# The two mixers of a long block: order of the weight columns, slots of the interleaved threads, buffers of retention's statistics

## What is computed

```
proj = h @ w_in        # hq hf hi hg (4 heads of 128) | rq rk (4 x 32) rv rg (256) | lx ly (256)
log_f = log(lb + (1-lb) sigmoid(hf));  k = (1-lb) sigmoid(-hf);  q = silu(hq) * 128**-0.5
o_hg  = rmsnorm(hgrn2(q, k, hi, log_f)) * silu(hg)          # 4 heads: gated linear recurrence
o_ret = head_groupnorm(retention(rope(rq), rope(rk), rv)) * silu(rg)
xc    = causal_conv4(lx)
o_lru = rg_lru(xc; sigmoid gates from two small matmuls of xc) * gelu(ly)
h    += concat(o_hg, o_ret, o_lru) @ w_out
```

## Time and profile before

| | us |
|---|---|
| time, median of 3 runs (2721.88 to 2722.41) | 2722.36 |
| the profiled execution's own time | 2721.52 |
| its span, first to last instruction | 2719.7 |
| TensorE busy | 2624.5 |
| VectorE busy | 1371.7 |
| ScalarE busy | 1053.1 |
| the mixers' tiles begin at (first, second) | 1354.35, 2041.12 |

### The profile page before, as it was taken

How to read it: one execution, slowest core, us unless ns; L and a number is a source line. 1 busy time by engine, 2 the same in 40 slices (tenths; PEclk the granted TensorE clock), 3 DMA queues, 4 the chain that set the end, 5 groups by cost and what they waited for, 6 DMA issues and landing times.

```text
span 2719.7 us, 42796 instructions
## 1 busy us (share of the span) xinstructions
PE 2624.5 (96%) x18948; PEld 2341.3 (86%) x18948; DVE 1371.7 (50%) x2195; ACT 1053.1 (39%) x1709; POOL 30.7 (1%) x69
## 2 busy tenths in 40 slices
PE   7999999999999999999999999999999899999998
PEld 5776888888877788888888889999998888999998
DVE  4766633324556643332666446555246644655523
ACT  3554522213444442221544344443234434443421
POOL 0000000000000000000000000000000000000000
PEclk9999999999999999999999999999999999999999
DMA  4221222232312122222311222222232122222222
GB/s 164 83 85 63 78 93 93 90 101 74 109 65 76 63 94 94 97 96 88 114 63 48 67 93 91 94 94 84 92 128 79 34 81 90 80 92 94 90 86 74
DMA packets 39467, 236.04 MB, mean 87 GB/s; under 512 B 5248, under 2 KB 7296, under 8 KB 17008
## 3 DMA queue, kind: packets, MB, share of 16 engines
q1 hardware_dynamic: 34336, 213.93, 23.3%
q0 software_dynamic: 3792, 17.26, 1.8%
q10 hardware_dynamic: 1152, 2.10, 0.2%
HBM read 222.65 MB, written 6.42 MB: 84 GB/s over the span
## 4 chain that ended last, share of the span: by engine, by line
PE 85%; DVE 8%; ACT 5%; DMA 1%; issue 1%; SPq 0%; ACTq 0%; DVEq 0%
PE P L505 72%; PE P L593 3%; PE P L615 2%; PE P L512 2%; DVE WL L1741 1%; ACT WH L1194 1%; PE P L870 1%; PE P L627 1%; PE P L641 1%; PE P L670 1%; PE P L956 1%; DVE X L2041 1%; DVE small L2044 1%; DMA X<-in_xT 0%; PE P L846 0%
## 5 line engine op out<-in xcount | busy, mean ns | idle before, releaser
L505 PE MATMUL P<-XH,WL 128*128 128x264 f32 (+2 forms) x3080 | 851.8, 325 | 34.5 <-DVE WL L1741 19.4
L505 PE MATMUL P<-XL,WH 128*128 128x264 f32 (+2 forms) x3080 | 825.4, 317 | 0.0
L505 PE MATMUL P<-XH,WH 128*128 128x264 f32 (+2 forms) x3080 | 823.6, 316 | 0.0
L1741 DVE TENSOR_TENSOR WL<-raw,WH 128x1024 fp32r<-128x1024 f32 (+1 forms) x404 | 483.8, 1201 | 533.8 <-ACT WH L1194 533.3
L1194 ACT ACTIVATE WH<-raw 128x1024 fp32r<-128x1024 f32 (+1 forms) x404 | 418.0, 1038 | 596.5 <-PE P L505 595.7
L505 PEld LDWEIGHTS P<-XH,WL 128*128 128x128 f32 x3080 | 521.6, 189 | 83.5 <-issue 19.0
L505 PEld LDWEIGHTS P<-XH,WH 128*128 128x128 f32 x3080 | 518.8, 189 | 38.3
L505 PEld LDWEIGHTS P<-XL,WH 128*128 128x128 f32 x3080 | 519.3, 189 | 35.3
L2374 DVE SCALAR_TENSOR_TENSOR tmp<-P,PP,tmp 128x527 f32<-128x527 f32 x88 | 67.4, 766 | 198.5 <-ACT tmp L1690 198.5
L505 PE MATMUL P<-GHH,WL 128*128 128x264 f32 x704 | 150.2, 284 | 0.0
L505 PE MATMUL P<-GHH,WH 128*128 128x264 f32 x704 | 149.6, 283 | 0.0
(11 more groups left out here) (335 smaller groups left out, 3460.5 us busy)
## 6 DMA issues: line engine op xcount, KB each, us to landing
raw<-in_wts SPq DMA_DIRECT2D x170, 1024.0 KB, 4.9
raw<-in_wts SPq DMA_DIRECT2D x32, 896.0 KB, 4.7
spill<-X POOLq DMA_DIRECT2D x2, 2112.0 KB, 9.0
X<-spill POOLq DMA_DIRECT2D x16, 264.0 KB, 4.2
tmp<-in_biasT POOLq DMA_DIRECT2D x16, 256.0 KB, 4.3
qswap<-qraw SPq DMA_DIRECT2D x44, 64.0 KB, 2.0
tab<-in_tR POOLq DMA_DIRECT2D x2, 1056.0 KB, 6.1
X<-in_xT ACTq DMA_DIRECT2D x8, 256.0 KB, 13.1
```

The source lines that it names most:

```text
L505: ins = nc.tensor.matmul(P[:, a:a + x1 - x0], wb[:, s, 128 * k:128 * k + 128], xb[:, kx, x0 - c0:x1 - c0], start=start and i == 0, stop=st ...
L1741: nc.vector.tensor_tensor(WL[:, u % NS, 0:length(u)], raw[:, u // 2 % RAW, a:a + length(u)], WH[:, u % NS, 0:length(u)].bitcast(F), ALU.su ...
```

## The change

It moves things and computes the same. The columns of LRU's input (lx0, lx1) are now the first two tiles, those of its output gate (ly0, ly1) stand ahead of head 3's and retention's gates. The heads have 14 steps, the norm's product and the gate's in two of them, and new slots; LRU runs at slots 10 to 60, its gate at 172 to 184; retention's scores have an empty step after the rope, and the gate of retention is a thread of its own, `ret_gate`, at 188 to 206. Retention's values and statistics lie in buffers of the heads (KBs, hK, Qs, hB, hA), with waits for head 3's last use of them. The output projection takes LRU's k-steps first and retention's last. X is loaded back in another order, at events of its own for each tile. The threads are called with `ret_gate` on all three engines (on TensorE it is idle).

```diff
@@ -18,9 +18,9 @@
 
 
 WIDE = ("v0", "v1", "rv")
-MIXER_TILES = [("v0", 20), ("hf1", 8), ("hq1", 8), ("hg1", 8), ("lx0", 8), ("lx1", 8), ("rq0", 8), ("rk1", 8),
-               ("hf2", 8), ("hq2", 8), ("v1", 20), ("hg2", 8), ("hf3", 8), ("hq3", 8), ("rv", 20), ("hg3", 8),
-               ("rg0", 8), ("rg1", 8), ("ly0", 8), ("ly1", 8)]
+MIXER_TILES = [("lx0", 8), ("lx1", 8), ("v0", 20), ("hf1", 8), ("hq1", 8), ("hg1", 8), ("rq0", 8), ("rk1", 8),
+               ("hf2", 8), ("hq2", 8), ("v1", 20), ("hg2", 8), ("hf3", 8), ("hq3", 8), ("rv", 20), ("ly0", 8),
+               ("ly1", 8), ("hg3", 8), ("rg0", 8), ("rg1", 8)]
 
 
 def mixer_column(name):
@@ -206,10 +206,11 @@
                 pass
 
 
-def mixer_threads(hgrn, lru, ret_scores, ret_values, lru_gate):
-
-    return Threads((hgrn(0), 13, 1, 46), (hgrn(1), 13, 46, 90), (hgrn(2), 13, 92, 136), (hgrn(3), 13, 138, 190),
-                   (lru(), 8, 52, 86), (ret_scores(), 5, 74, 108), (ret_values(), 9, 157, 193), (lru_gate(), 3, 190, 204))
+def mixer_threads(hgrn, lru, ret_scores, ret_values, lru_gate, ret_gate):
+
+    return Threads((hgrn(0), 14, 1, 52), (hgrn(1), 14, 54, 96), (hgrn(2), 14, 98, 136), (hgrn(3), 14, 138, 184),
+                   (lru(), 8, 10, 60), (ret_scores(), 6, 78, 114), (ret_values(), 8, 157, 187), (lru_gate(), 3, 172, 184),
+                   (ret_gate(), 3, 188, 206))
 
 
 def one(b):
@@ -340,8 +341,7 @@
         hseq = [X[:, 6 + n, :] for n in range(2)]
         rraw, RQ, RK = (X[:, 0, :], X[:, 1, :]), X[:, 2, :], X[:, 3, :]
         KTr = X[:, 4, 0:512]
-        ro, rsq = (X[:, 4, :], X[:, 5, :]), X[:, 3, :]
-        tmp_rs = [X[:, n, :] for n in range(2)]
+        ro, rsq, tmp_rs = (KBs[0], KBs[1]), (hK, Qs[0]), (hB, hA)
         rgate = (rstd[:, :], tmp[3])
 
         pe_done, act_done, dve_done, pool_done = (semaphore(n + "_done") for n in ("pe", "act", "dve", "pool"))
@@ -476,11 +476,9 @@
                 for h in range(2, 4):
                     pool.wait_ge(*at("ht", l, h - 1))
                     nc.gpsimd.memset(hB[:, :], 1.0).then_inc(*pool.up("hB", l, h))
-                for k in (2, 0, 1, 3, 4, 5, 6, 7):
-                    if k == 2:
-                        pool.wait_ge(*at("rpv", l, 1))
-                    else:
-                        pool.wait_ge(*at("gl", l, max(k, 5)))
+                for k, event in ((0, ("rt", l)), (1, ("rt", l)), (3, ("rt", l)), (5, ("rt", l)), (4, ("rkv", l, 1)), (2, ("rpv", l, 1)),
+                                 (6, ("gl", l, 6)), (7, ("gl", l, 7))):
+                    pool.wait_ge(*at(*event))
                     nc.gpsimd.dma_start(X[:, k, :], spill[:, k, :]).then_inc(x_back[k], 16)
 
 
@@ -1040,6 +1038,7 @@
                     ones_sum(perm_r, rraw[n], two(3), True, True).then_inc(*pe.up("rperm", l, n))
                     give((6, 7), ("rrope1", l, n))
                     yield
+                yield
                 for n in range(2):
                     pe.wait_ge(*at("rrope", l, 1))
                     take(4, 5, 6, 7)
@@ -1106,13 +1105,13 @@
                 for n in range(2):
                     pe.wait_ge(*at("ro", l, n))
                     take(6, 7)
-                    ones_sum(ones_ret, ro[n], two(3), True, True).then_inc(*pe.up("rmean", l, n))
+                    ones_sum(ones_ret, ro[n][:, :], two(3), True, True).then_inc(*pe.up("rmean", l, n))
                     give((6, 7), ("rcen", l, n))
                     yield
                 for n in range(2):
                     pe.wait_ge(*at("rsq", l, n))
                     take(6, 7)
-                    ones_sum(ones_ret, rsq, two(3), True, True).then_inc(*pe.up("rvar", l, n))
+                    ones_sum(ones_ret, rsq[n][:, :], two(3), True, True).then_inc(*pe.up("rvar", l, n))
                     give((6, 7), ("rl", l, n))
                     yield
                 yield
...
@@ -1141,11 +1141,11 @@
                         tile(U + u, two(p), XH, XL, slot)
                         give((2 * p, 2 * p + 1), (name[:2], l, int(name[2])))
                 UO = first[f"mo{l}"]
-                out_first(UO, works, GH, GL, (0, 1, 2, 4, 5, 3), [two(0), two(1)], ("gl", l), 0)
+                out_first(UO, works, GH, GL, (0, 1, 2, 6, 7, 3), [two(0), two(1)], ("gl", l), 0)
 
                 def tiles(m, r):
                     if m < 2:
-                        finish_tile(UO + m, r, GH, GL, (6, 7), ("gl", l), 0)
+                        finish_tile(UO + m, r, GH, GL, (4, 5), ("gl", l), 0)
                     else:
                         tile(UO + m, r, GH, GL)
 
@@ -1567,7 +1567,7 @@
                 yield
 
             def ret_scores(l):
-                for _ in range(4):
+                for _ in range(5):
                     yield
                 act.wait_ge(*at("rt", l))
                 nc.scalar.activation(KTr[:, 0:384], P[:, 2560:2944], ACT.Copy).then_inc(*act.up("rkt0", l))
@@ -1579,23 +1579,27 @@
                 yield
                 for n in range(2):
                     act.wait_ge(*at("rpv", l, n))
-                    nc.scalar.activation(ro[n], pair_bank(3), ACT.Copy).then_inc(*act.up("ro", l, n))
-                    yield
-                act.wait_ge(*at("rcen", l, 0))
-                nc.scalar.activation(rsq, ro[0], ACT.Square).then_inc(*act.up("rsq", l, 0))
-                yield
-                yield
+                    act.wait_ge(*at("ht", l, 3))
+                    nc.scalar.activation(ro[n][:, :], pair_bank(3), ACT.Copy).then_inc(*act.up("ro", l, n))
+                    yield
+                for n in range(2):
+                    act.wait_ge(*at("rcen", l, n))
+                    act.wait_ge(*at("hp", l, 3, 7))
+                    nc.scalar.activation(rsq[n][:, :], ro[n][:, :], ACT.Square).then_inc(*act.up("rsq", l, n))
+                    yield
                 for n in range(2):
                     act.wait_ge(*at("rvar", l, n))
+                    act.wait_ge(*at("hst", l, 3, 3))
                     nc.scalar.preload_act_table_set("natural_log_exp_and_others")
-                    nc.scalar.activation(tmp_rs[n], pair_bank(3), ACT.Ln, bias=eps6).then_inc(*act.up("rl", l, n))
+                    nc.scalar.activation(tmp_rs[n][:, :], pair_bank(3), ACT.Ln, bias=eps6).then_inc(*act.up("rl", l, n))
                     act.wait_ge(*at("rl", l, n))
-                    nc.scalar.activation(tmp_rs[n], tmp_rs[n], ACT.Exp, scale=-0.5).then_inc(*act.up("rex", l, n))
-                    if n == 0:
-                        act.wait_ge(*at("rcen", l, 1))
-                        nc.scalar.activation(rsq, ro[1], ACT.Square).then_inc(*act.up("rsq", l, 1))
+                    nc.scalar.activation(tmp_rs[n][:, :], tmp_rs[n][:, :], ACT.Exp, scale=-0.5).then_inc(*act.up("rex", l, n))
+                    yield
+
+            def ret_gate(l):
+                for n in range(2):
                     act.wait_ge(*at("rgm", l, n))
-                    nc.scalar.activation(GH[:, 4 + n, :], ro[n], ACT.Copy).then_inc(*act.up("gh", l, 4 + n))
+                    nc.scalar.activation(GH[:, 4 + n, :], ro[n][:, :], ACT.Copy).then_inc(*act.up("gh", l, 4 + n))
                     yield
                 yield
 
...
@@ -2326,24 +2333,42 @@
                 yield
                 for n in range(2):
                     dve.wait_ge(*at("rmean", l, n))
-                    nc.vector.tensor_tensor(ro[n], ro[n], pair_bank(3), ALU.subtract).then_inc(*dve.up("rcen", l, n))
-                    yield
-                for n in range(2):
-                    dve.wait_ge(*at("rex", l, n))
-                    nc.vector.scalar_tensor_tensor(ro[n], ro[n], par("retn", l), tmp_rs[n], ALU.mult, ALU.mult
-                                                   ).then_inc(*dve.up("rnr", l, n))
+                    nc.vector.tensor_tensor(ro[n][:, :], ro[n][:, :], pair_bank(3), ALU.subtract).then_inc(*dve.up("rcen", l, n))
+                    yield
+                yield
+                scaled(l, 0)
+                yield
+
+            def scaled(l, n):
+                dve.wait_ge(*at("rex", l, n))
+                dve.wait_ge(*at("rsq", l, n))
+                nc.vector.scalar_tensor_tensor(ro[n][:, :], ro[n][:, :], par("retn", l), tmp_rs[n][:, :], ALU.mult, ALU.mult
+                                               ).then_inc(*dve.up("rnr", l, n))
+
+            def ret_gate(l):
+                def gated(n):
                     dve.wait_ge(*at("rnr", l, n))
                     dve.wait_ge(*at("rg", l, n))
-                    nc.vector.tensor_tensor(ro[n], ro[n], rgate[n], ALU.mult).then_inc(*dve.up("rgm", l, n))
+                    nc.vector.tensor_tensor(ro[n][:, :], ro[n][:, :], rgate[n], ALU.mult).then_inc(*dve.up("rgm", l, n))
+
+                def low(n):
                     dve.wait_ge(*at("gh", l, 4 + n))
-                    nc.vector.tensor_tensor(GL[:, 4 + n, :], ro[n], GH[:, 4 + n, :].bitcast(F), ALU.subtract).then_inc(*dve.up("gl", l, 4 + n))
-                    yield
```

(15 more changed lines are left out.)

## The result

The changed kernel takes **2702.24 us** (median of 6 runs, 2700.78 to 2703.69); the kernel before took 2722.12 beside it (6 runs). The ratio is 0.9927, 95% interval 0.9914 to 0.9940: 19.9 us less, against 18 forecast (2704.3).

A forecast was written before the change was run, and what follows sets the result against it. TensorE, busy 96% of the span, bounds the kernel, so only its idle time and lower clock can change: 24.2 us a mixer gone, 15.2 brought in, 18 gained in both, giving 2704.3 us; own range 2695 to 2713.

The forecast's parts named there:

- nine kinds of waits: TensorE's waits in the mixers of the kernel before, 35.4 us in all, 17.7 a mixer, nearly all ending on VectorE or ScalarE.
- Item 1: LRU's convolution and gate between head 0's levels: TensorE waits 1.7 us a mixer, between 0 and 4.
- Item 2: LRU's second gate ahead of head 1's first level: 19.2 us chain against TensorE's 14.0, wait 5.2, between 0 and 8.
- Item 3: Lower clock after the wait at head 1's first level: 3.4 us lost a mixer, between 1.8 and 5.
- Item 4: Heads 2 and 3: nothing at head 2's levels, 0.9 us a mixer at head 3's, between 0 and 2.
- Item 5: Mixer's end: waits of 0.45 us at retention's first mean, 2.6 at its second variance, and 0.9 of clock.
- The sum: Per mixer 15.2 us brought in against 24.2 gone: gain 9.0, 18 in both mixers.
- The signs: Waits left at head 1's first level, retention's second variance, head 3's first level; ScalarE without gap; VectorE waiting for it twice.
- no pile would form before head 1: Rival: TensorE finds head 1's first level ready, 8.6 us more come back a mixer, 2687 us; chance 0.17.
- the crowd would only move: Rival: VectorE is behind through heads 0 and 2 too, 9 us a mixer, time 2722 us; chance 0.19.
- Slower by the clock: Rival: clock stays low after head 1's first level, for all of slots 60 to 92 2732 us; chance 0.09.

The follow-up runs named there:

- e5: Changed kernel with LRU at slots 10 to 64 in place of 60, on VectorE only; 2697.35 us, 0.9907 of the kernel before.
- e13: Changed kernel with LRU's exponential replaced by a tanh, one table load less (computes something else); 2699.40 us, 0.9917 of the kernel before.
- e8: Changed kernel with all eight tiles of X reloaded only when retention's second low part is written; 2703.80 us, 0.9931 of the kernel before.
- e3: Changed kernel with LRU at slots 10 to 64 in place of 60, on all engines; 2704.86 us, 0.9934 of the kernel before.
- e6: Changed kernel with head 1 at slots 58 to 98 in place of 54 to 96; 2704.47 us, 0.9936 of the kernel before.
- e7: Changed kernel with retention's values at slots 157 to 191 in place of 187; 2700.86 us, 0.9920 of the kernel before.
- e9: Changed kernel with head 1 at slots 58 to 98, head 3 at 139 to 185, retention's values at 157 to 191; 2702.09 us, 0.9925 of the kernel before.
- e11: e5 with head 1 at slots 54 to 100 in place of 96; 2697.86 us, 0.9909 of the kernel before.

## Why the prediction was right

- **Method.** The gain was sought in TensorE's idle time and its clock alone. Shown: the same matmuls, 11.0 us less idle, 9.8 less busy.
- **What goes.** The nine kinds of waits went as told, but for head 3's first level. (There was a tenth, of 0.4 us a mixer, for the eviction of hf; 0.3 of it stayed.) The clock they cost was mis-sized: 6.5 us a mixer. The stretches of the first mixer gave 7.0; I had not read those of the second, three of 20 us (of the busy times, TensorE's alone is shown):

```profile
2100.00:2120.00 20.00, 16.50 (x215) 0.91 0.04 15
...
2140.00:2160.00 20.00, 16.66 (x159) 0.83 0.16 54
...
2260.00:2280.00 20.00, 14.57 (x94) 0.83 0.40 134
```

  That is 20 x (0.09 + 0.17 + 0.17) = 8.6.
- **Item 1**, LRU inside head 0: 1.7 foretold, 1.0 + 0.7 + 0.4 = 2.1 measured, at the three places named.
- **Item 2**, head 1's first level: 5.2 foretold, 5.7 measured. The chain was 19.5 in place of 19.2. Of the 0.3, 0.1 is a link that I read wrongly: load, silu and cast of hq1 stand in the sum with 2.75, and the rows that it names give 1401.17 - 1398.32 = 2.85. e5 and e13 show that it is this chain: with hK ahead of LRU's products the wait is gone, and with one load less it is 1.4 shorter.
- **Item 3**, the clock after it: 3.4 foretold; 3.4 measured in the first mixer, 3.6 in the second.
- **Item 4**: head 3's first level 0.9 foretold, 1.4 measured; head 2 nothing, and nothing.
- **Item 5**: 0.45 and 2.6 foretold, 0.5 and 2.6 measured. From the end of head 3's sum (1555.29) to the second variance (1566.28) it took 11.0 us, as counted link by link, and TensorE was there after 8.4, as counted. Clock 0.9 foretold, none in this execution, 3.4 in the first mixer of e8's and none in its second.
- **The sum**: 15.2 a mixer brought in; measured 2.1 + 5.7 + 3.4 + 1.4 + 0.5 + 2.6 = 15.7 in the first, 15.9 in the second. Gone: 24.7 in the first mixer, 26.3 in the second. 9.0 + 10.4 = 19.4 us, of the 20.7 between the two profiled executions (2721.52 and 2700.78); 1.3 I can't place (the clock is read to a hundredth, which leaves up to 0.1 us open in each stretch). That the forecast is within 2 us of the result is in part luck: the waits brought in were 1.4 us a mixer more than foretold (12.3 against 10.9), the clock lost with them 0.7 to 0.9 less (3.4 and 3.6 against 4.3), and 0.5 and 2.1 us more of clock came back than the 6.5.
- **The signs.** The waits came where they were named and none was for a weight. ScalarE did not run quite without a gap: it waited 0.57 us for the head's gate product before its high part (1408.01), a gap that the count of item 2 has in it (ScalarE through at 6.9, VectorE at 7.6). VectorE waited there for ScalarE four times, not twice: 6.29 us for the Exp, 0.71 for the high part, 4.18 for LRU's sigmoid and 1.96 for its exponential.
- **The rivals.** That no pile would form before head 1 was refuted by the 5.7. That the crowd would only move was not so for this change, but it is what happened to four of my own repairs (e3, e6, e7, e9) and in part to e5 and e11. The reason I gave against it, that VectorE does less than its slots allow, counts VectorE's work and forgets its waits for ScalarE, which the experiments brought among the levels. Slower by the clock: refuted, the clock was back at 1.00 from 1440 on, 20 us after the wait.

My expectations of the repairs were worse than the forecast of the change: I foretold 8 to 17 us for e3, e5, e6 and e9 and got none to 5. In the forecast I had walked through every step of the new table on every engine; for the repairs I worked out only the wait aimed at. What stays open: whether head 1's pile can be had back at all (seven loads of tables lie on ScalarE between slots 44 and 60, and putting functions of one table together wasn't tried).

## What to carry to other kernels

In a kernel whose engines take their steps by a hand-written table, a wait can be worked out to half a microsecond: take the chain from the last instruction on the full engine, add its links queue by queue (loads of tables and casts included), and compare with the k-steps between. Then look at what a shift moves its steps past, on every queue. Here four shifts of whole threads (e3, e6, e7, e9) gave nothing, and in e6 and e7 a step moved behind others on VectorE took back what was won. An empty step that lengthens one distance and keeps every order gave 5.2 us of waits and 6.5 of time. A reordering on one queue alone (e5) cut a long wait in pieces: it gave 4.4 us of waits in both mixers and, in sum, no clock.

## What the runs showed of the hardware

A wait of the same length does not always cost the same clock. At the 2.6 us wait of retention's second variance in the first mixer the stretch had 1.00 in the changed kernel and 0.83 in e8. These two kernels have the same waits in the mixers, but 2614.7 against 2620.9 us of busy time for the same matmuls, and 2700.78 against 2706.88 us for the two profiled executions. Single executions of one kernel differ by such steps (2700.78 to 2703.69 for the changed kernel), so a difference of 2 to 3 us between single executions of these kernels says nothing.
